# Router of a hierarchical mixture of experts: top two picked tile by tile, slot and coefficient rows sent through device memory

## The reference

```python
xn = rms_norm(x, norm2_g).reshape(bsz * t, d)
lg = xn @ rg_w + rg_b                     # 4 groups
p_group = softmax(lg); p_top, grp = top_k(p_group, 1)
le = (xn @ re_w + re_b).reshape(-1, 4, 8)  # 32 experts
le_sel = le of the group grp
top_l, top_i = top_k(le_sel, 2)
w_top = softmax(top_l) * p_top
for e in range(32):                        # combine: w_top at the two picked experts
    hdn = silu(xn @ w_gate[e]) * (xn @ w_up[e])
    out = out + combine[:, e:e+1] * (hdn @ w_down[e])
x = x + out; final RMSNorm
```

## Time and profile before

| | us |
|---|---|
| median of 3 runs | 843.48 (843.28 to 843.7) |
| the profiled execution | 843.39 |
| its span in the profile | 841.6 |
| granted TensorE clock, mean over the span | 0.979 |

### The profile page before, as it was taken

The page is one execution under the profiler, slowest core; times in us unless marked ns, Lnnn a source line. Parts: engine busy times, 40 slices in busy tenths (PEclk is TensorE's granted clock), DMA queues, the critical chain, the costliest instruction groups (busy, mean ns, idle before and its releaser), DMA issues.

```text
span 841.6 us, 21589 instructions
## 1 busy us (share of the span) xinstructions
PE 775.0 (92%) x8655; PEld 591.7 (70%) x8656; DVE 427.2 (51%) x1142; ACT 324.3 (39%) x562; POOL 259.1 (31%) x132
## 2 busy tenths in 40 slices
PE   4999999999999999999999979999898889989964
PEld 4999999999999999865555545555555545545532
DVE  3156977999994244153444333445343334434424
ACT  4432767564345833253323322323322223222224
POOL 3846699978577778200000000000000000000000
PEclk9999999999999999989999999999999999999997
DMA  7734343435454746963899999999999999999992
GB/s 254 229 106 145 101 151 100 151 100 160 129 180 158 280 150 241 339 278 151 340 422 423 421 422 422 422 421 422 422 422 421 422 422 422 421 422 423 421 421 119
DMA packets 53173, 249.99 MB, mean 297 GB/s; under 512 B 6600, under 2 KB 6600, under 8 KB 28562
## 3 DMA queue, kind: packets, MB, share of 16 engines
q1 hardware_dynamic: 49760, 246.95, 74.1%
q10 hardware_dynamic: 3377, 2.57, 1.2%
HBM read 246.76 MB, written 2.75 MB: 296 GB/s over the span
## 4 chain that ended last, share of the span: by engine, by line
PE 62%; DMA 18%; DVE 11%; SPq 4%; ACT 2%; issue 2%; ACTq 1%; DVEq 0%
PE bank L1450 24%; DMA piece<-in_exp_w_up 17%; PE bank L1621 12%; DVE bank L1065 7%; PE bank L1650 7%; PE bank L1572 5%; PE bank L1609 4%; PE bank L1448 4%; SPq L549 4%; PE bank L1637 1%; DVE sq L1127 1%; PE bank L1579 1%; PE bank L1519 1%; DMA stage<-in_norm_g 1%; PE bank L1513 1%
## 5 line engine op out<-in xcount | busy, mean ns | idle before, releaser
L603 POOL TENSOR_TENSOR w_lo<-raw,w_hi 128x2048 fp32r<-128x2048 f32 x39 | 180.5, 4631 | 62.6 <-ACT w_hi L728 62.5
L1621 PE MATMUL bank<-piece,xe 128*32 128x256 f32 x2816 | 169.5, 392 | 32.1 <-DMA piece<-in_exp_w_up 26.3
L1621 PEld LDWEIGHTS bank<-piece,xe 128*32 128x32 f32 x2816 | 97.7, 113 | 98.0 <-issue 47.5
L1450 PE MATMUL bank<-x_hi,w_hi 128*128 128x384 f32 x432 | 145.4, 337 | 0.3 <-DVE ua L1084 0.2
L1450 PE MATMUL bank<-x_hi,w_lo 128*128 128x384 f32 x432 | 144.4, 334 | 0.0
L1450 PE MATMUL bank<-x_lo,w_hi 128*128 128x384 f32 x432 | 144.4, 334 | 0.0
L1065 DVE SCALAR_TENSOR_TENSOR bank<-ub,vec,bank 128x256 f32<-128x256 f32 (+1 forms) x416 | 137.2, 419 | 0.0
L1296 DVE SCALAR_TENSOR_TENSOR silu_and_hid<-bank,few,silu_and_hid 64x256 f32<-64x256 f32 x44 | 21.5, 490 | 170.4 <-ACT silu_and_hid L914 170.4
L728 ACT ACTIVATE w_hi<-raw 128x2048 fp32r<-128x2048 f32 x39 | 74.8, 1919 | 74.8 <-PE bank L1450 71.2
L1650 PE MATMUL bank<-piece,hidT 128*32 128x256 f32 x1408 | 94.2, 384 | 5.5
L1450 PEld LDWEIGHTS bank<-x_hi,w_hi 128*128 128x128 f32 x432 | 81.1, 188 | 1.4 <-DVE ua L1084 0.5
(11 more groups left out here) (239 smaller groups left out, 1009.9 us busy)
## 6 DMA issues: line engine op xcount, KB each, us to landing
piece<-in_exp_w_down SPq DMA_DIRECT2D x64, 1024.0 KB, 26.6
piece<-in_exp_w_gate SPq DMA_DIRECT2D x64, 1024.0 KB, 25.9
piece<-in_exp_w_up SPq DMA_DIRECT2D x64, 1024.0 KB, 26.9
raw<-in_w_in SPq DMA_DIRECT2D x28, 1024.0 KB, 5.2
raw<-in_w_out_a SPq DMA_DIRECT2D x4, 1024.0 KB, 5.0
raw<-in_w_out_b SPq DMA_DIRECT2D x4, 1024.0 KB, 5.3
raw<-in_w_o SPq DMA_DIRECT2D x4, 1024.0 KB, 5.0
out<-n_out SPq DMA_DIRECT2D x3, 512.0 KB, 3.3
```

Of the source, the lines that this page charges most:

```text
L603: pool.tensor_tensor(w_lo[u % NW][:, :, :], raw[u % NW][:, :, :], w_hi[u % NW][:, :, :].bitcast(F32), ALU.subtract).then_inc(lo_ready, 1)
L1450: ins = pe.matmul(b, wp[:, k % UK, cols], xp[:, k, :], start=start, stop=stop)
L1621: last = pe.matmul(GU[q * T:(q + 1) * T, :], xe[:, k, :], wide(pairs[q // 2], k)[:, q % 2 * QE:(q % 2 + 1) * QE], start=(k == 0), stop=(k ...
```

## The change

The picks are written tile by tile; each step waits only for the step before it of the same tile. Steps of two tiles alternate. The exponentials are started one by one. The coefficients are computed ahead of reading the counts. `values` is one array of 18 columns (slots 6, the reciprocal root twice, coefficients 6); ACT writes columns 6 to 17 and then 0 to 5 to a tensor `value_rows` in device memory, turned, and reads the rows back with a broadcast over partitions. `turn_values`, `spread` and their copies are gone. GpSimd's clearing waits for the reads. The seeds stand elsewhere. The logit products, the counting, the expert loop and its weights are as before.

```diff
-    AUX += [("turned", 0, "act"), ("spread", 0, "act"), ("spread", 1, "act"), ("order", 0, "dve")]
-    AUX += [("turned", 1, "act"), ("spread", 2, "act"), ("spread", 3, "act")]
+    AUX += [("order", 0, "dve")]
...
-        values = [scratch(3 * NT), scratch(2 * NT)]
+        values = scratch(6 * NT)
+        rstd2, rstd2_too, coefs = values[:, 2 * NT:3 * NT], values[:, 3 * NT:4 * NT], values[:, 4 * NT:6 * NT]
+        value_rows = nc.dram_tensor("value_rows", (6 * NT, P), F32)
...
-            wait_aux_read(pool, aux("spread", 3))
+            pool.wait_ge(tables_ready, 1)
+            pool.wait_ge(value_rows_in, 48)
             pool.memset(y_hi[:].bitcast(F32), 0.0).then_inc(y_ready, 1)
...
+            act.wait_ge(exp_in, 1)
+            act.activation(gexp, gexp, ACT.Exp).then_inc(exp_out, 1)
             act.wait_ge(exp_in, 2)
-            act.activation(gexp, gexp, ACT.Exp).then_inc(exp_out, 1)
             act.activation(dexp, dexp, ACT.Exp).then_inc(exp_out, 1)
...
-            read_aux(aux("turned", 0))
+            def rows_to_all(rows, r0, r1, c0):
+
+                act.dma_start(flat[rows, c0:c0 + (r1 - r0) * P],
+                              value_rows[r0:r1, :].rearrange("(a r) p -> a (r p)", a=1)
+                              .to_broadcast([rows.stop - rows.start, (r1 - r0) * P])).then_inc(value_rows_in, 16)
+
+            act.wait_ge(coefs_ready, 1)
+            act.dma_start(value_rows[2 * NT:6 * NT, :].rearrange("r p -> p r"), values[:, 2 * NT:6 * NT],
+                          allow_slow_non_contiguous=True).then_inc(coefs_out, 16)
+            act.wait_ge(slots_ready, 1)
+            act.dma_start(value_rows[0:2 * NT, :].rearrange("r p -> p r"), values[:, 0:2 * NT],
+                          allow_slow_non_contiguous=True).then_inc(slots_out, 16)
+            act.wait_ge(coefs_out, 16)
+            rows_to_all(slice(0, P // 2), 2 * NT, 4 * NT, 2 * N)
+            rows_to_all(slice(P // 2, P), 4 * NT, 6 * NT, 2 * N)
             copy_rows(1)
-            for a in ("spread", 0), ("spread", 1), ("turned", 1), ("spread", 2), ("spread", 3):
-                read_aux(aux(*a))
+            act.wait_ge(slots_out, 16)
+            rows_to_all(slice(0, P), 0, 2 * NT, 0)
             act.wait_ge(tables_ready, 1)
...
             dve.reciprocal(rstd2, small[:, 8:8 + NT]).then_inc(rstd_ready, 1)
             dve.wait_ge(rstd_ready, 1)
+            dve.tensor_copy(rstd2_too, rstd2).then_inc(rstd_ready, 1)
...
-            first_max(lg[:, :, 0:NG], NG, gmax, ghot, t0[:, :, 0:NG])
...
-            first_max(le, NE, top[0], hot[0], t0)
-            link(dve.scalar_tensor_tensor(le, hot[0], -BIG, le, ALU.mult, ALU.add))
-            first_max(le, NE, top[1], hot[1], t0)
-            dve.tensor_tensor(both_b, hot[0], hot[1], ALU.add).then_inc(masks_ready, 1)
...
+            def best(i, c):
+                ready(i)
+                done(i, dve.tensor_reduce(top[c][:, i:i + 1], le[:, i, :], AX.X, ALU.max))
...
+            read_logits(2)
+            best_group(2)
+            mark_hot(1, 0)
+            group_ranks(2)
+            without_first(1)
+            first_group(2)
+            best(1, 1)
+            other_groups(2)
+            ranks(1, 1)
+            in_group(2)
+            first(1)
+            best(2, 0)
+            mark_hot(1, 1)
+            ranks(2, 0)
+            both_hot(1)
+            first(2)
+            dve.tensor_tensor(gexp, lg[:, :, 0:NG], gmax.unsqueeze(2).to_broadcast([P, NT, NG]), ALU.subtract)\
+               .then_inc(exp_in, 1)
+            mark_hot(2, 0)
+            without_first(2)
+            best(2, 1)
+            ranks(2, 1)
+            dve.tensor_tensor(dexp, top[1], top[0], ALU.subtract).then_inc(exp_in, 1)
+            first(2)
+            dve.wait_ge(exp_out, 1)
+            dve.tensor_reduce(sum_exp, gexp, AX.X, ALU.add).then_inc(dve_chain, 1)
+            chain[0] += 1
+            mark_hot(2, 1)
+            both_hot(2)
+
+            dve.wait_ge(exp_out, 2)
+            link(dve.scalar_tensor_tensor(inverse, dexp, 1.0, sum_exp, ALU.add, ALU.mult))
+            link(dve.reciprocal(inverse, inverse))
+            link(dve.tensor_tensor(coefs[:, 0:NT], inverse, rstd2, ALU.mult))
+            dve.wait_ge(rstd_ready, 2)
+            dve.tensor_tensor(coefs[:, NT:2 * NT], coefs[:, 0:NT], dexp, ALU.mult).then_inc(coefs_ready, 1)
...
-            wait_aux_read(dve, aux("spread", 3))
+            dve.wait_ge(value_rows_in, 48)
...
-            wait_aux_read(pe, aux("logit", NT - 1))
+            wait_aux_read(pe, aux("logit", 0))
             seed(1, 0)
+            wait_aux_read(pe, aux("logit", 1))
             seed(1, 1)
-            seed(2, 0)
-            pe.wait_ge(masks_ready, 1)
             b = start_aux(aux("pos"))
             for i in range(NT):
+                pe.wait_ge(masks_ready, i + 1)
...
-            seed(2, 1)
+            wait_aux_read(pe, aux("logit", 2))
+            seed(2, 0)
             pe.wait_ge(counts_ready, 1)
             b = start_aux(aux("table"))
             end_aux(pe.matmul(b[:, 0:NE], ones_b[0:NE, :], in_front, start=True, stop=True))
-            seed(0, 1)
...
+            seed(2, 1)
...
-            pe.wait_ge(slots_ready, 1)
-            turn_values(0)
             pe.wait_ge(picked, 1)
             pe.wait_ge(x_rows_ready, NT)
             gather()
-            wait_aux_read(pe, aux("turned", 0))
-            spread(0)
-            spread(1)
-            pe.wait_ge(rows_ready, 1)
-            turn_rows()
             pe.wait_ge(order_ready, 2)
...
-            pe.wait_ge(coefs_ready, 1)
-            turn_values(1)
-            wait_aux_read(pe, aux("turned", 1))
-            spread(2)
-            spread(3)
+            seed(0, 1)
+            pe.wait_ge(rows_ready, 1)
+            turn_rows()
+            seed(0, 0).then_inc(combined, 1)
             pe.wait_ge(tables_ready, 1)
...
-            wait_aux_read(pe, aux("spread", 3))
-            seed(0, 0).then_inc(combined, 1)
```

More of the change, by code:

```diff
@@ L1168, in _, with ready, done, read_logits @@
             dve.wait_ge(rstd_ready, 1)
-            for i in range(NT):
+            dve.tensor_copy(rstd2_too, rstd2).then_inc(rstd_ready, 1)
+            at = [0] * NT
+            def ready(i):
+                dve.wait_ge(dve_chain, at[i])
+            def done(i, ins):
+                chain[0] += 1
+                at[i] = chain[0]
+                ins.then_inc(dve_chain, 1)
+            def read_logits(i):
                 a = aux("logit", i)
@@ new lines, in first, with mark_hot, without_first @@
+            def first(i):
+                ready(i)
+                done(i, dve.tensor_reduce(rank_of[:, i:i + 1], t0[:, i, :], AX.X, ALU.max))
+            def mark_hot(i, c):
+                ready(i)
+                done(i, dve.tensor_scalar(hot[c][:, i, :], t0[:, i, :], rank_of[:, i:i + 1], None, ALU.is_equal))
+            def without_first(i):
+                ready(i)
+                done(i, dve.scalar_tensor_tensor(le[:, i, :], hot[0][:, i, :], -BIG, le[:, i, :], ALU.mult, ALU.add))
@@ new lines, in both_hot @@
+            def both_hot(i):
+                ready(i)
+                dve.tensor_tensor(both_b[:, i, :], hot[0][:, i, :], hot[1][:, i, :], ALU.add).then_inc(masks_ready, 1)
+            dve.wait_ge(consts, 11)
+            read_logits(0)
+            best_group(0)
+            group_ranks(0)
+            first_group(0)
+            other_groups(0)
+            in_group(0)
+            best(0, 0)
+            ranks(0, 0)
+            first(0)
+            read_logits(1)
+            best_group(1)
@@ new lines, in _ @@
+            mark_hot(0, 0)
+            group_ranks(1)
+            without_first(0)
+            first_group(1)
+            best(0, 1)
+            other_groups(1)
+            ranks(0, 1)
+            in_group(1)
+            first(0)
+            best(1, 0)
+            mark_hot(0, 1)
+            ranks(1, 0)
+            both_hot(0)
+            first(1)
[4 more added lines that the diff above has]
+            without_first(1)
```

80 lines of the change are left out of this document (31 added, 49 removed).

## The result

| | us |
|---|---|
| the changed kernel, median of 6 runs | 858.35 (848.44 to 860.82) |
| the kernel before, beside it | 843.59 (843.21 to 844.72) |
| ratio | 1.0146, 95% interval 1.0119 to 1.0173 |
| the profiled execution after, and its span | 860.82, 859.1 |
| forecast | 838.7, range 836.2 to 841.9 |

The change costs 14.8 us where a gain of 4.7 was forecast, far outside the range. The first page of the profile after, its first two parts, gives no hint of a cause: the engines did the same work in a longer span.

What follows compares the result with a forecast made beforehand. The end was taken as the moment the expert-weight stream becomes continuous, plus a constant, following item 0. Silu at item 0, 391.75 before, would come 4.7 us earlier: 843.4 - 4.7 = 838.7 us, range 836.2 to 841.9.

Steps and rivals of the forecast that it cites:

- part four: Values written to device memory and read back: writes 4.9 and 4.35 us, round trip last at item 0, Silu at 387.05.
- slot write: Write of 768 single slot numbers to device memory on ACT's queue: 4.35 us, landed at 380.9.
- slot read: Read of 393 KB repeating slot rows over partitions: 3.6 us, back at 384.5.
- The last hole: SyncE's queue waiting for item 3 before the weight stream is continuous: would end near 412.5 instead of 417.2.
- Rival (c): Slot read queues behind SyncE's three megabytes of weights, 7.5 us: Silu 2.8 us later than before, total 846.1; chance 0.09.
- The estimate drawn from its figure of 2.0 us: Slot write at 2.0 us plus descriptors: round trip about 2 us shorter, total about 837.3.
- Part one: Logits to first pick: tile-by-tile picks end at 372.84, table matmul not before 375.25; gain 1.5 us.
- Part two: Gather to item 0: 8.12 us falls to 4.57 without transposes, spreading matmuls and ACT copies; gain 3.55 us.
- Part three: Item 0's gate and up products, 4.76 us before: clock stays up with seeds close together; gain 1.1 us.
- up from 375.6 on: Sign to look for in the profile: the clock up from 375.6 us on; low beyond 376 would make the number wrong.
- Rival (b): Clock stays low until item 0: gain only 2.2 us, total 841.2, or 840 if low part of the time; chance 0.18.
- The frame: Item 0 sets when SyncE's last hole ends, and that hole sets the kernel's end.

Runs made afterwards that it cites:

- the second profile: Profile of the changed kernel run again, with TensorE's loop bounds kept at zero or above as the only edit: 855.93 us, ratio 1.0131.
- e9: Whole-rows version with coefficients turned before `seed(2, 0)`, their reads ahead of the slots' turning, `seed(2, 1)` behind the order's matmuls: 839.25 us, ratio 0.9944.
- e3: Changed kernel with SyncE sending the last three megabytes of first weights only after all three row reads have landed: 850.43 us, ratio 1.0065.
- the last version: e9 with `seed(2, 1)` moved back behind the table, ahead of the slots' turning: 837.55 us, ratio 0.9933.

## Why the prediction was wrong

**The step that failed is part four, the price of the write.** It said that nothing in the trace writes single numbers, took 4.9 us for 1536 and 4.35 for 768, and allowed 8 at most. They took 14.0 and 16.8. The 4.9 was a good price for so many pieces, as the runs with 32 and 64 bytes between them show (4.4 to 4.8); what the nearest row, a load of 16-byte pieces, could not show is that a write of pieces that lie side by side has a price of its own. The 8 was a guess with no row behind it, and the range was built as if it were a limit. The steps to Silu at item 0, forecast 387.05:

| term | taken | measured | later by |
|---|---|---|---|
| slots ready to write issued | 376.57 | 377.22 | 0.65 |
| slot write | 4.35 | 16.8 | 12.45 |
| slot read | 3.6 | 10.7 | 7.1 |
| the coefficient instruction, table, Silu | 2.55 | 2.5 | 0 |

These make the 20.15 us between 387.05 and 407.20. The last hole ended 434.46 - 412.5 = 22.0 later than forecast, so 1.85 came behind Silu: from there to the hole's end it took 27.26 us, and 25.46 before. That fits the lower clock behind the waits (0.50 from 404.8 to 413), but no run took it apart.

**Rival (c) came true as well**, by its own mechanism and near its price: 7.5 us for the weights ahead, against 10.7 - 5.1 = 5.6 on the read and 5.5 to 7.9 in the median. Its chance of 0.09 hung on a write landing 0.9 us late, and on nothing in the trace; with no row for the write, that was far too sure. It was not the cause of the sign, though: without it the kernel is still at 850.43. It also met what the prediction had against it, the small load that landed in 4.9 beside weights: that was 16 KB, this is 384. In the same stretch of the trace before, the load of the experts' router weights, 128 KB on ACT's queue, took 7.1 us.

**The rule of the Trainium skill** that the prediction weighed (a strided last dimension becomes one descriptor per element, rearrange it) was right in its advice. The estimate drawn from its figure of 2.0 us, 837.3, was wrong as the other was, since it counted descriptors and not where they land. Followed instead of costed, the rule gives the version with whole rows, at 837.45; that this lies beside 837.3 is chance, since the estimate was for the turned write.

**Part one, picks:** in direction. The marks' last step, at 373.84, ended at 374.03, not 372.84. Steps of tiles 0 and 1 were still standing in front of the third logits: these were read at 370.09, and the first step on them started at 370.37, 0.83 later than the 369.54 before. The 15 steps from there took 3.66 us instead of 3.3, 0.25 apart on average where 0.22 was taken, with other tiles' steps between them. The table matmul came at 375.86 instead of 375.25. Alone, that gain is worth nothing in the total (843.53).

**Part two, gather to item 0:** right in kind and too long by about a microsecond, where the round trip lets it be seen: 382.13 - 378.03 = 4.10 and 381.60 - 377.80 = 3.80 with whole rows and without turning; 4.57 + 0.4 was forecast. In the changed kernel the cover that I had costed at 0.4, the copy behind the coefficients' wait, cost 9.8.

**Part three, the clock:** up at item 0 in those versions (3.66 for its products), down in the changed kernel (5.50), behind a wait of 9.06 us. The sign "up from 375.6 on" failed as well: in the changed kernel the clock was 1.00 from 374 to 375.7 but 0.50 from 377 to 378, ahead of the long waits, and its gather took 2.20 us instead of 1.50; the second profile shows the same, and why stays open. Not every fall had a wait in front of it: in the trace before, the clock went from 1.00 to 0.50 between 368.5 and 369 while the narrow logit matmuls followed each other without a gap. Rival (b)'s mechanism showed in the run with `seed(2, 1)` moved (e9), at 1.8 us.

**The frame:** right. 417.21 moved by 17.25 and the end by 17.5; with whole rows the hole moved by -5.24 and the profiled execution by 838.41 - 843.39 = -4.98. 838.7 is within 1.5 us of the two kernels whose writes land quickly (837.45 and 837.23), partly by the luck told above.

**Open:** why the change's runs spread over 12 us (848.44 to 860.82) where the kernel before spreads over 2. Both its profiles have the slot read just behind the weights; that the faster runs had it ahead would fit the 5.5 to 7.9 us, but no profile caught one, and it can't be all: with the meeting taken away (e3) the runs still spread from 848.78 to 854.08, where a narrow spread had been expected. Nor was it followed up why the slot read of the last version was issued 2.6 us after its write where a bound of 1.55 was seen.

## What to carry to other kernels

A turned write to device memory, one number per piece, is priced by where the numbers land: at 32 bytes or more from each other 1536 of them took 4.4 to 4.8 us, side by side 14 to 15, and at a pitch of 8 KB between rows 44. Turn on TensorE first and write whole rows, 2 us. Small transfers that something waits for have to be issued ahead of bulk loads on other queues, here by half a microsecond, and before a wait is removed one asks what it had been holding back: here moving one copy ahead of a wait sent three megabytes into the slow writes and cost about 4 us more.

## What the runs showed of the hardware that was not expected

- Single numbers written side by side: the prices in the table above, up to ten times (43.8 against 4.4) and thirteen times (65.3 against 4.9) those of the same pieces apart; half as many could take longer (16.8 against 14.0), issued while the first write was still under way.
- Such a write goes with slow ones beside it: megabytes issued into it took 15.8 and 22.0 us to land, with DMA engines 0.90 busy at 40 GB/s.
- A read of 384 KB, repeated over partitions, took 3.4 to 5.1 us when issued 0.56 us or more ahead of three megabytes on another engine's queue, and 7.6 to 10.7 when issued with the first of them (0.08 us ahead) or behind it; 14.3 where the slow writes were in it too.
- Independent small VectorE instructions of two tiles stood 0.10 to 0.17 us apart (369.33, 369.44, 369.56 ahead of the third logits), dependent ones of the third tile 0.22 to 0.29 at its end.
